# A two-layer hybrid block in f32: scan products on full tiles, and layer 1's down projection in seven products

## The reference

```python
def _wkv_scan(r, w, k, v, kk, a, s0, reverse):
    def step(S, inp):
        r_t, w_t, k_t, v_t, kk_t, a_t = inp
        sa = jnp.einsum('bhvk,bhk->bhv', S, kk_t)
        S = (S * w_t[:, :, None, :] - sa[..., None] * (kk_t * a_t)[:, :, None, :]
             + v_t[..., None] * k_t[:, :, None, :])
        return S, jnp.einsum('bhvk,bhk->bhv', S, r_t)
...
def _mlp(h, w1, w2):
    return jnp.square(jax.nn.relu(h @ w1)) @ w2
```

## Time and profile before

| what | us |
|---|---|
| median of 3 runs (lowest, highest) | 2406.4 (2401.8, 2408.0) |
| the profiled execution's own time | 2408.26 |
| its span, first to last instruction | 2406.5 |
| TensorE busy, matmuls | 2362.7 |
| VectorE busy | 1075.4 |
| ScalarE busy | 602.9 |
| GpSimd busy | 348.2 |

### The profile page before, as it was taken

One profiled execution on the slowest core, in us unless ns is written; L12 is line 12 of the kernel. 1 busy time (PEld: TensorE's weight loads), 2 busy tenths in 40 slices (PEclk: granted clock), 3 DMA queues, 4 the chain that ended last, 5 costly groups with the idle time before them and its releaser, 6 DMA issues.

```text
span 2406.5 us, 48804 instructions
## 1 busy us (share of the span) xinstructions
PE 2362.7 (98%) x21774; PEld 1617.1 (67%) x21774; DVE 1075.4 (45%) x1988; ACT 602.9 (25%) x1248; POOL 348.2 (14%) x249
## 2 busy tenths in 40 slices
PE   8999999999999999999999999999999999999998
PEld 5554564455556554458888887566577767788887
DVE  3452334243555542137876875431546566421101
ACT  3353323132232321011000002441333334211100
POOL 0000000000101100026666671010000011000000
PEclk9999999999999999999999999999999999999999
DMA  8101111213231113232224565112121212245443
GB/s 307 53 18 70 45 61 44 96 63 110 95 107 39 45 46 115 78 123 97 88 88 149 189 243 194 53 71 89 53 89 64 64 61 66 81 149 175 155 152 105
DMA packets 64543, 239.99 MB, mean 100 GB/s; under 512 B 7024, under 2 KB 8064, under 8 KB 63440
## 3 DMA queue, kind: packets, MB, share of 16 engines
q1 hardware_dynamic: 61824, 220.23, 26.6%
q0 software_dynamic: 2512, 16.66, 1.9%
HBM read 235.81 MB, written 1.05 MB: 98 GB/s over the span
## 4 chain that ended last, share of the span: by engine, by line
PE 89%; DVE 5%; DMA 2%; issue 1%; ACT 1%; SPq 0%; DVEq 0%; ACTq 0%
PE psum L430 87%; PE psum L769 2%; DMA normed<-panels 1%; DVE normed L2348 1%; DVE normed L2345 1%; DMA arena<-panels 1%; DVE arena L2329 0%; SPq L2712 0%; ACT arena L811 0%; DVE arena L1492 0%; ACT normed L719 0%; ACT arena L821 0%; DVE arena L1509 0%; DVE arena L1507 0%; DVE arena L1235 0%
## 5 line engine op out<-in xcount | busy, mean ns | idle before, releaser
L430 PE MATMUL psum<-normed,panel_ring 128*128 128x256 f32 (+1 forms) x2880 | 973.5, 484 | 3.0 <-DVE arena L1235 1.1
L430 PEld LDWEIGHTS psum<-normed,panel_ring 128*128 128x128 f32 x2880 | 530.2, 190 | 318.9 <-issue 265.8
L430 PE MATMUL psum<-arena 64*64 64x64 f32 (+6 forms) x14040 | 608.2, 251 | 20.1 <-issue 9.0
L430 PEld LDWEIGHTS psum<-arena 64*64 64x64 f32 (+3 forms) x14040 | 431.6, 139 | 251.6 <-issue 180.9
L430 PE MATMUL psum<-arena,panel_ring 128*128 128x256 f32 (+1 forms) x2048 | 550.4, 422 | 0.0
L430 PEld LDWEIGHTS psum<-arena,panel_ring 128*128 128x128 f32 x2048 | 384.3, 190 | 125.2 <-issue 81.4
L786 DVE TENSOR_REDUCE softmax_stats<-psum 128x1 f32<-128x512 f32 (+1 forms) x144 | 83.7, 599 | 171.6 <-PE psum L430 170.3
L811 ACT ACTIVATE arena<-psum,softmax_stats 128x512 f32<-128x512 f32 (+1 forms) x144 | 87.6, 612 | 211.8 <-PE psum L769 102.5
L1235 DVE SCALAR_TENSOR_TENSOR arena<-arena,psum 128x512 f32<-128x512 f32 (+1 forms) x64 | 35.3, 553 | 152.8 <-PE psum L430 145.3
L1220 ACT ACTIVATE arena<-psum 128x512 f32<-128x512 f32 (+1 forms) x64 | 31.4, 490 | 216.1 <-PE psum L430 216.0
L1728 POOL COPY arena<-arena 128x512 f32<-128x512 f32 x16 | 21.3, 1356 | 440.8 <-PE psum L430 431.1
(11 more groups left out here) (215 smaller groups left out, 1872.5 us busy)
## 6 DMA issues: line engine op xcount, KB each, us to landing
panel_ring<-panels SPq DMA_DIRECT2D x350, 512.0 KB, 3.5
normed<-panels SPq DMA_DIRECT2D x40, 512.0 KB, 3.7
arena<-panels SPq DMA_DIRECT2D x24, 512.0 KB, 12.0
arena<-small_b POOLq DMA_DIRECT2D x2, 2176.0 KB, 8.9
arena<-bias_d POOLq DMA_DIRECT2D x2, 2048.0 KB, 8.9
arena<-x_t SPq DMA_DIRECT2D x2, 1024.0 KB, 7.1
arena<-x_t POOLq DMA_DIRECT2D x1, 2048.0 KB, 10.6
arena<-const_r POOLq DMA_DIRECT2D x2, 800.0 KB, 6.3
```

What stands on the lines that cost most here:

```text
L430: return nc.tensor.matmul(out, lhsT, rhs, start=start, stop=stop, skip_group_check=check)
```

## The change

Three edits go together.

1. **Scan by full products.** G of the two heads is written as two diagonal blocks of a 128x128 matrix (`g_scan`, in `m13`) and the state too (`p_states`, two buffers of two directions, 128x128); the blocks beside are zero. GpSimd sets these zeros: `states` once per layer, those of `m13` in each pair after the last level (`places_set`, for which TensorE now waits before the scan). One scan step has, for each direction, one product of 128 columns for G·state and one of 64 columns for the outputs, in place of four small ones each. VectorE writes each head's block by itself: the copies of G, per direction and four chunks, go from one operation to two, a first state is written by four new operations, and a scan step has four operations of 64x64 for two of 128x64. Q lies in `X` now.
2. **Join and fill.** JOIN is 4. The H products are split over two steps; the y products of the join come after `h_full`, with the second. In ticks with a step of `close` or of the next `prep`, half of the fill is taken ahead of it.
3. **Layer 1's down projection in seven products.** `stage_mlp_down7` replaces `stage_mlp`. The up projection stays, but VectorE makes from the squares the sums that seven products need. The down projection is 16 units, each of 2 panels; a unit makes 7 products of 4 blocks, each 128 columns wide. Four units add up to a group of two output tiles. For each unit GpSimd makes three sums of weight blocks and VectorE two, all 128x512. After a group, ScalarE copies two banks and VectorE joins the parts and adds them to `x` in halves.

```diff
-PREP, RAW, LEVEL_STEPS, JOIN, SCAN, CLOSE = 17, 4, 2 * (LEVELS - 1), 3, NCH - 1, 8
+PREP, RAW, LEVEL_STEPS, JOIN, SCAN, CLOSE = 17, 4, 2 * (LEVELS - 1), 4, NCH - 1, 8
...
-        aw, pu, gq, hs, states = halves(bk), halves(Le), m13, kt, X
+        aw, pu, hs, q_scan = halves(bk), halves(Le), kt, X
+        g_scan = m13.rearrange("p d c a t -> p d c (a t)")
+        states = at["p_states"]
...
-            e.wait_ge(gq_ready.h, gq_ready.at(1))
-            for c in y_chunks:
-                for d, hd in units:
-                    t = tside(d, hd)
-                    mm(yb[d][half[hd], token(c)], pu[t, d, c, 1, :], m4[t, d, c, :], False, False, check=True)
             for n, (src, right) in enumerate(((kt, vt), (bt, pu[:, :, :, 1, :]))):
+                if n == 0:
+                    e.wait_ge(gq_ready.h, gq_ready.at(1))
                 for c in range(NCH):
                     for d, hd in units:
                         t = tside(d, hd)
                         if c != order[d][-1]:
                             p = mm(psum[half[hd], d, token(c)], src[t, d, c, :], right[t, d, c, :], n == 0 and c == 0, n == 1, check=True)
-            p.then_inc(h_full.h, 1)
-            yield
+                if n == 1:
+                    p.then_inc(h_full.h, 1)
+                    for c in y_chunks:
+                        for d, hd in units:
+                            t = tside(d, hd)
+                            mm(yb[d][half[hd], token(c)], pu[t, d, c, 1, :], m4[t, d, c, :], False, False, check=True)
+                yield
             e.wait_ge(h_ready.h, h_ready.at(1))
             e.wait_ge(gq_ready.h, gq_ready.at(2))
+            e.wait_ge(places_set.h, places_set.at(2))
             for i in range(1, NCH):
-                now = lambda d: states[:, d, i, :] if i > 1 else hs[:, d, order[d][0], :]
                 if i > 1:
                     e.wait_ge(s_ready.h, s_ready.at(i - 1))
                 if i < NCH - 1:
-                    for d, hd in units:
-                        p = mm(psum[half[hd], i % 2, d * CHUNK:(d + 1) * CHUNK], gq[half[hd], d, order[d][i], 0, :], now(d)[half[hd]], True, True)
+                    for d in range(2):
+                        p = mm(psum[:, i % 2, d * P:(d + 1) * P], g_scan[:, d, order[d][i], :], states[:, i % 2, d, :], True, True)
                     p.then_inc(s_full.h, 1)
                 if with_y(order[0][i]):
-                    for d, hd in units:
+                    for d in range(2):
                         c = order[d][i]
-                        p = mm(yb[0][half[hd], token(c)], now(d)[half[hd]], gq[half[hd], d, c, 1, :], False, False, check=True)
+                        p = mm(yb[0][:, token(c)], states[:, i % 2, d, :], q_scan[:, d, c, :], False, False, check=True)
                 if i == NCH - 1:
                     p.then_inc(y_full.h, 1)
                 yield
...
+            if ft == 0:
+                if attended is not None:
+                    e.wait_ge(attended[0].h, attended[0].at(attended[1]))
+                nc.gpsimd.memset(states.rearrange("p n d k -> p (n d k)"), 0.0)
...
+            e.wait_ge(c_full.h, c_full.at(LEVELS - 1))
+            for hd in range(2):
+                p = nc.gpsimd.memset(m13[half[hd], :, :, 1 - hd, :].rearrange("p d c t -> p (d c) t"), 0.0)
+            p.then_inc(places_set.h, 1)
```

VectorE's part of the join and the scan:

```diff
                 for d in range(2):
-                    p = nc.vector.tensor_tensor(gq[:, d, part, 0, :], pieces(n)[:, d, :, 0, :], wide(eye, 4), ALU.add)
+                    for hd in range(2):
+                        p = nc.vector.tensor_tensor(m13[half[hd], d, part, hd, :], pieces(n)[half[hd], d, :, 0, :], wide(eye[half[hd]], 4), ALU.add)
                     if with_y(4 * n):
-                        p = nc.vector.tensor_tensor(gq[:, d, part, 1, :], pieces(n)[:, d, :, 1, :], ar[:, d, part, 1, :], ALU.add)
+                        p = nc.vector.tensor_tensor(q_scan[:, d, part, :], pieces(n)[:, d, :, 1, :], ar[:, d, part, 1, :], ALU.add)
                 p.then_inc(gq_ready.h, 1)
             yield
+            yield
             e.wait_ge(h_full.h, h_full.at(1))
-            for d, cs, steps in ((0, slice(0, 7), slice(0, 7)), (1, slice(3, None, -1), slice(0, 4)), (1, slice(7, 4, -1), slice(4, 7))):
+            for d, hd in units:
+                nc.vector.tensor_scalar(states[half[hd], 1, d, half[hd]], psum[half[hd], d, token(order[d][0])], dcol_i[half[hd], 0, d:d + 1],
+                                        None, ALU.mult)
+            for d, cs, steps in ((0, slice(1, 7), slice(1, 7)), (1, slice(2, None, -1), slice(1, 4)), (1, slice(7, 4, -1), slice(4, 7))):
                 n = steps.stop - steps.start
                 p = nc.vector.tensor_tensor(hs[:, d, cs, :], chunked(psum[:, d, :])[:, cs, :],
                                             dcol_i[:, steps, d:d + 1].broadcast_to([P, n, CHUNK]), ALU.mult)
@@ -1799,9 +1818,10 @@
             for i in range(1, NCH):
                 if i < NCH - 1:
                     e.wait_ge(s_full.h, s_full.at(i))
-                    for d in range(2):
-                        p = nc.vector.scalar_tensor_tensor(states[:, d, i + 1, :], psum[:, i % 2, d * CHUNK:(d + 1) * CHUNK],
-                                                           dcol_i[:, i, d:d + 1], hs[:, d, order[d][i], :], ALU.mult, ALU.add)
+                    for d, hd in units:
+                        p = nc.vector.scalar_tensor_tensor(states[half[hd], (i + 1) % 2, d, half[hd]],
+                                                           psum[half[hd], i % 2, d * P + hd * CHUNK:d * P + (hd + 1) * CHUNK],
+                                                           dcol_i[half[hd], i, d:d + 1], hs[half[hd], d, order[d][i], :], ALU.mult, ALU.add)
                     p.then_inc(s_ready.h, 1)
```

The down projection on TensorE, its weight sums on GpSimd and VectorE, and the join of a group (the plain form's lines that it replaces are those of `stage_mlp` above):

```diff
+        opens = lambda u: u % 4 == 0
+        closes = lambda u: u % 4 == 3
...
+            def product(u, out, lhs, part, opening, begins=False):
+                for k in range(4):
+                    p = mm(out, lhs[:, k, :], hid[:, 4 * (u % 4) + k, part, :], opening and k == 0, closes(u) and k == 3, check=True)
+                    if begins and k == 0:
+                        p.then_inc(panels_begun.h, 1)
+                return p
+
+            for u in range(NU):
+                at_first = P_DOWN + 8 * (u // 4) + u % 4
+                loaded[u] = stream.take(l, at_first), stream.take(l, at_first + 4)
+            for u in range(NU):
+                v, x2, x5, x1 = u // 4, wx[:, u % 2, 1], wx[:, u % 2, 2], wx[:, u % 2, 0]
+                (w1, _, _), (w2, _, _) = loaded[u]
+                if v == 0:
+                    e.wait_ge(hid_ready.h, hid_ready.at(summed_at(4 * u + 3)))
+                if opens(u) and v >= 2:
+                    e.wait_ge(emptied.h, emptied.at(v - 1))
+                e.wait_ge(weights.h, weights.at(3 * u + 1))
+                product(u, bank(v, 0)[:, 1, :], x2, 0, opens(u))
+                e.wait_ge(shared.h, shared.at(2 * u + 1))
+                product(u, bank(v, 1)[:, 0, :], x5, 3, opens(u))
+                p = product(u, bank(v, 0)[:, 0, :], w1[:, 0:4, :], 1, False, begins=True)
+                if closes(u):
+                    p.then_inc(m3_full.h, 1)
+                e.wait_ge(shared.h, shared.at(2 * u + 2))
+                product(u, bank(v, 2)[:, 0, :], w1[:, 4:8, :], 6, opens(u))
+                e.wait_ge(weights.h, weights.at(3 * u + 3))
+                p = product(u, bank(v, 1)[:, 1, :], w2[:, 4:8, :], 2, False, begins=True)
+                if closes(u):
+                    p.then_inc(m4_full.h, 1)
+                p = product(u, bank(v, 2)[:, 1, :], w2[:, 0:4, :], 5, False)
+                if closes(u):
+                    p.then_inc(m67_full.h, 1)
+                product(u, m1_bank(v), x1, 4, opens(u)).then_inc(m1_done.h, 1)
+                yield
...
+        def pool(e):
+            yield from idle(8 * N_UP)
+            for u in range(NU):
+                (w1, _, _), (w2, _, _) = loaded[u]
+                arrived(e, u)
+                nc.gpsimd.tensor_tensor(wx[:, u % 2, 1], w2[:, 0:4, :], w2[:, 4:8, :], ALU.add).then_inc(weights.h, 1)
+                nc.gpsimd.tensor_tensor(w2[:, 0:4, :], w2[:, 0:4, :], w1[:, 0:4, :], ALU.subtract).then_inc(weights.h, 1)
+                nc.gpsimd.tensor_tensor(wx[:, u % 2, 0], w1[:, 0:4, :], w2[:, 4:8, :], ALU.add).then_inc(weights.h, 1)
+                yield
...
+            def weight_sums(u):
+                (w1, _, _), (w2, _, _) = loaded[u]
+                arrived(e, u)
+                nc.vector.tensor_tensor(wx[:, u % 2, 2], w1[:, 0:4, :], w1[:, 4:8, :], ALU.add).then_inc(shared.h, 1)
+                e.wait_ge(shared.h, shared.at(2 * u + 1))
+                nc.vector.tensor_tensor(w1[:, 4:8, :], w1[:, 4:8, :], w2[:, 4:8, :], ALU.subtract).then_inc(shared.h, 1)
...
+                if j in (29, 31):
+                    weight_sums((j - 29) // 2)
...
+            def join(v):
```

(28 more changed lines are left out.)

130 lines of the change are left out of this document (82 added, 48 removed).

## The result

The changed kernel takes 2429.05 us in the median of 4 runs (2424.43 to 2430.91), the kernel before, timed beside it, 2407.22 (2401.82 to 2408.17): a ratio of 1.0092, with an interval from 1.0071 to 1.0114. It is **slower** by 22 us or 0.9%, with the whole interval above 1, where 2410.3 us was forecast with a range of 2395 to 2421. The profiled execution took 2424.43 us.

What follows compares the result with a forecast made beforehand. TensorE was taken as the bound, busy 2362.7 of 2406.5 us, plus what it waits for. Terms -9.0 + 0.3 + 2.7 + 8.7 + 1.2 = +3.9 us gave 2412.2 profiled, 2410.3 us against the median; range 2395 to 2421.

Steps and rivals of the forecast that it cites:

- down projection: Layer 1's down projection: 896 records at 0.1117 us replace 512, -10.4 us, with a longer tail and waits -9.0 us.
- join split by fill: Join: splitting the H products adds one more going over to small tiles, 0.34 us in each of 8 pairs, +2.7 us.
- TensorE's full products: Scan on TensorE: full steps go from 0.82 to 0.89 us, G or y alone from 0.57 to 0.45, +0.3 us.
- copies of G, first state in halves: VectorE before the scan: more copies cost +1.3 us and first states 0.8 per pair, covered in the join.
- four scan operations: VectorE's scan steps: four operations for two lengthen TensorE's waits, +8.7 us in layer 1 and +1.2 in layer 0.
- the earlier preparation: Scan on VectorE: JOIN = 4 puts the next pair's preparation one scan step earlier; 11.2 us of preparation and branches becomes 11.6.
- the row with 2 columns: Trace row of full tiles with 2 columns, 0.10 us each, taken to show weight load decides y's cost: 0.45 us.
- rival B: Scan backlog worse than summed: VectorE's four operations queue behind preparation, 4 us more in each layer, 2416 to 2422; chance 0.17.
- Two of those now take 0.39 us until the next starts: VectorE's scan step: two operations' 0.39 us doubles to 0.78 for four, +0.39 us in each of 6 steps.
- covered by the H products and the fill: Join: VectorE's extra copy and first-state operations, +1.3 and 0.8 us per pair, hide beside TensorE's work and cost nothing.

Runs made afterwards that it cites:

- e1: The kernel before with only the seven-product down projection and its buffers, JOIN = 3, scan and join as before: 2394.87 us, ratio 0.9956.
- e4: The kernel before with the seven-product down projection, JOIN = 4, the split join and the change's fill; scan and copies as before: 2400.82 us, ratio 0.9990.
- e9: e8 with G's copies and the first state also back over 128 partitions in two operations each (recurrence result wrong): 2402.25 us, ratio 0.9992.
- e8: The changed kernel with VectorE's scan step as two operations over 128 partitions, TensorE's products untouched (recurrence result wrong): 2410.73 us, ratio 1.0034.
- e10: The changed kernel with all four scan operations of a step on the first 64 partitions, same number and order (recurrence result wrong): 2416.62 us, ratio 1.0052.
- e11: The changed kernel itself, unaltered, timed again beside e9 and e10: 2435.58 us, ratio 1.0128.
- e7: The seven-product down projection alone plus block-diagonal G, stacked 64-column states, two VectorE operations per step, outputs in each step on small tiles: 2416.72 us, ratio 1.0054.

## Why the prediction was wrong

The ladder of kernels gives each term of the sum a measured price, from ratios times 2405 us. Every step of it but the first goes from one sitting to another.

| term | forecast | measured | between |
|---|---|---|---|
| down projection | -9.0 | -10.6 | before and `e1` |
| join split by fill | +2.7 | +8.2 | `e1` and `e4` |
| TensorE's full products | +0.3 | +0.5 | `e4` and `e9` |
| copies of G, first state in halves | 0, covered | +10.1 | `e9` and `e8` |
| four scan operations | +9.9 | +14.0 and +22.6 | `e8` and the change, both timings |
| sum | +3.9 | +22 and +31 | |

The intervals are some 0.001 to each side for the runs with many rounds and 0.002 for the others, so a single term is known to 3 to 5 us, and each takes in what the clock did. The 9.9 forecast for the four operations also held what the earlier preparation would bring. Within one sitting, `e4` to `e8` (full products, copies, first state) is 10.6 us, `e9` to `e10` (copies, first state, two more operations in each step) 14.4, and `e10` to `e11` (the crossings alone) 18.3.

**Right.** The down projection, in its size and its parts: 0.1117 us a record, GpSimd's sums hidden. TensorE's scan, in `e9`:

```profile
1943.89 1.00 PE L430 MATMUL psum<-arena 128*128 128x128 f32 x8
1944.73 1.51 PE L430 MATMUL psum<-normed,panel_ring 128*128 128x256 f32 x6
1946.08 0.55 PE L430 MATMUL psum<-arena 128*128 128x64 f32 x4
1946.47 1.51 PE L430 MATMUL psum<-normed,panel_ring 128*128 128x256 f32 x6
```

Four records of y with 64 columns take 0.39 us until the fill starts, four of G 0.45 (1929.12 to 1929.57), and record by record both stand 0.11 apart. A full step costs 2.19 - 6 x 0.2158 = 0.90 us (1943.89 to 1946.08), the 0.89 of the forecast, for 0.82 before. So a full tile with 64 columns costs what one with 128 does, as the row with 2 columns said; that it is the weight load that decides is the reading left, not one that was tested. The rule of the Trainium skill, TensorEngine Tiling (Array Packing), section Instruction Overhead, by which these products would have been half as dear, is not borne out by these rows. The mechanism of the loss, too, was the one named: in layer 1 VectorE runs without a gap from scan step 2 on, and TensorE waits for the line that replaced 1803 in 14 places, 15.7 us in place of 3.2: 11 of them in layer 1, 13.5 us, and 3 in layer 0, 2.2 us. It is rival B's mechanism at over B's price. Two slips of addition in the prediction change nothing: 11.2 - 0.7 + 1.2 is 11.7, and 8 us on top of 2410.3 is 2418.

**The step that failed** is "Two of those now take 0.39 us until the next starts", and so "four 0.78: +0.39 us in each of 6 steps". The spacing of 0.19 us was read from two operations that lie on the same 128 partitions, and carried over to four that alternate between two halves. Measured until the next starts: 0.78 us with four on one half, 1.21 with four that alternate. From first to last, 0.85 us for four on one half (0.28 + 3 x 0.19), 0.98 with one crossing between halves, 1.18 with three. A crossing thus costs 0.11 to 0.13 us each over an overlapped start; the operation after it starts as the one before it ends, 0.30 us on (0.28 is its own length). The Trainium skill, VectorE: DVE Perf Modes, section "Two Vector instructions with no wait between them", has this as a model: an instruction is held until all earlier ones of the engine have finished when its input or output starts in another quadrant of 32 partitions than the last one's. The three durations agree with it; the forecast was made without it. With 1.21 for 0.78 in each step VectorE's share of the stretch of layer 1 is 16.3 + 6 x 0.43 = 18.9 us, and 18.55 was measured. Longer waits follow from there.

**The second** is the sentence that the copies and the first state are "covered by the H products and the fill". By size it weighs as much: 0 for some 10 us, where the first is off by 4 and 13 in the two timings. By the same spacing across halves the copies start 0.42 to 0.44 us apart, not a third of one, and they end 2.0 us later (4.25 less 2.21), some 8 x 2.0 = 16 us of VectorE in all. What I named as cover was TensorE's work beside them, but two readers stand behind them on TensorE's queue: the next pair's head sums, which need the result of the last copy (0.55 us at 1932.65), and the scan's start. The waits that the profile puts down to the copies are 2.3 us in 4 places. From `e9` to `e8` TensorE's idle time grows by 4.9 us; the rest of the 10 is about what the mean clock of their executions makes (below). I had asked what is behind VectorE's scan operations and not what is behind its copies.

**The third** is the split at 0.34 us a pair. Its own price was about right (an estimated 2.8 us, for 12 goings over and not 8), but it moves the next pair's preparation against the core's work, and that brought waits for ScalarE's tanh (1.7 us in 2 places) and more for the scan operations (5.2 for 3.2). That the preparation comes a step earlier I had in the sum of VectorE only.

**The clock** is on top. At 1947.52 TensorE has two records left, then waits 2.83 us; the granted clock of the stretches before and after its next start (1950.94), as busy times:

```profile
1947.52:1950.94 3.42, 0.59 (x3) 0.19 (x1) 3.35 (x8) 2.24 (x6) 0.00 (x0) 0.99 0.42 146
1950.94:1954.98 4.04, 4.04 (x15) 3.36 (x15) 3.86 (x9) 0.15 (x2) 0.00 (x0) 0.59 0.03 10
```

It falls to 0.59 of full, so 1.2 GHz for most of the stretch, just when TensorE is due to catch up. In `e11` it is at 0.51 for 6.8 us behind the wait at the same place. Such stretches, summed over the profile's record of the clock, are 30.1 us in the change as first profiled and 52.3 in `e11`; 31.7 in the kernel before, 29.0 in `e1`, 41.4 in `e8`, 25.6 in `e9`, 17.4 in `e4`. So in the first profile the clock has no part in the distance to the kernel before. Between the two timings of the change it has nearly all of it. At half the clock 22.2 us more cost 11.1, and the two profiled executions are 12.1 us apart (2424.43 and 2436.50), with the same waits for the scan operations (15.7 and 15.1 us). All executions say the same by their mean granted clock: 0.9928 over the four of the first timing and 0.9900 over those of `e11`, which over 2430 us is 6.7 us, and their mean times are 6.7 apart (2428.4 and 2435.1).

| kernel | TensorE idle in its profile, us | mean granted clock of its executions |
|---|---|---|
| `e9` | 43.9 | 0.9960 |
| `e8` | 48.8 | 0.9943 |
| `e10` | 51.4 | 0.9943 |
| the change, first timing | 58.3 | 0.9928 |
| the change, `e11` | 60.2 | 0.9900 |

Each 0.001 of the clock is an estimated 2.4 us. `e11` stands 18 us above `e10`: 8.8 are idle time, and 0.0043 of the clock makes 10. In this ladder the kernels that wait more also have the lower clock, so that a wait costs more than its own length, by an amount that differs from one execution to the next. That the waits bring the clock down is argued, not shown. `e7` has 49.0 us idle and 0.9925, and in `e11` the clock also falls at 1940.5, where the waits before it (0.55, then 0.27 us) are those that the first profile has too. Why it fell more in the last sitting stays open.

## What to carry to other kernels

Before an operation over 128 partitions is cut into pieces on fewer, read how far apart such pieces really start: pieces on the same partitions overlapped here (0.19 us apart), pieces that alternated between halves did not (0.30), and ordering them half by half took the four from 1.18 to 0.98 us and was 0.0028 and 0.0064 of the time below the two timings of the change (in other sittings; against the first the intervals overlap). Halving TensorE's instruction count by zeros beside the data bought nothing, since a record on a full tile cost 0.11 us whatever its columns, and the small ones that it replaced, with the going over to them and back, cost no more (0.82 us a full step, 0.90 after); and it handed the work to the engine that set the pace. For each operation that gets longer ask who waits for its result on the pacing engine, not only what runs beside it.
